# Nine gather slots and two weight slots in a two-layer decoder trunk with product-key expert retrieval

## The reference

```
h = RMSNorm(x);  z = h @ W_in
branches: differential attention, multi-head latent attention, short gated convolution
x += W_out( sum_i sigmoid(gate_i) * (branch_i @ W_branch_i) )
x += PEER(RMSNorm(x))
x += sigmoid(RMSNorm(x) @ W_pg) * (p[layer] @ W_pp)
```

## Time and profile before

| | |
|---|---|
| median of 3 runs | 3571.02 us (3570.99 to 3576.33) |
| the profiled execution | 3578.64 us, its span 3576.8 us |
| TensorE busy | 2852.6 us, 80% |
| VectorE busy | 2525.4 us, 71% |
| POOL, ScalarE busy | 37%, 35% |
| moved by DMA | 1296.91 MB, of it 1073.81 MB gathers and 221.31 MB plain loads |
| mean rate of the DMA | 363 GB/s over the span |

### The profile page before, as it was taken

How to read it: one execution, slowest core, us unless ns; L and a number is a source line. 1 busy time by engine, 2 the same in 40 slices (tenths; PEclk the granted TensorE clock), 3 DMA queues, 4 the chain that set the end, 5 groups by cost and what they waited for, 6 DMA issues and landing times. The chain is left out here.

```text
span 3576.8 us, 28034 instructions
## 1 busy us (share of the span) xinstructions
PE 2852.6 (80%) x8032; PEld 1460.7 (41%) x8032; DVE 2525.4 (71%) x5193; ACT 1263.9 (35%) x3352; POOL 1338.6 (37%) x1033
## 2 busy tenths in 40 slices
PE   8899787778998778777998778878998776557556
PEld 4554634435436334433436334535445432112112
DVE  1411577787777989787767979787767987777775
ACT  2320225456123344456213334447213232223222
POOL 0000033345433444345433443345433344554552
PEclk9989898889999999989999999989999997778777
DMA  4224389899999999999999999899999999999996
GB/s 159 105 83 155 110 339 381 346 415 417 421 421 376 408 410 413 376 403 421 421 418 377 390 411 404 341 406 417 421 421 381 365 409 421 421 422 399 422 422 254
DMA packets 182970, 1296.91 MB, mean 363 GB/s; under 512 B 20384, under 2 KB 21920, under 8 KB 28192
## 3 DMA queue, kind: packets, MB, share of 16 engines
q0 software_dynamic: 147456, 1073.81, 73.2%
q1 hardware_dynamic: 35360, 221.31, 15.7%
HBM read 1292.94 MB, written 2.10 MB: 362 GB/s over the span
## 5 line engine op out<-in xcount | busy, mean ns | idle before, releaser
L595 POOL DMA_INDIRECT ring<-in_uv,experts x1024 | 1336.1, 1305 | 2190.8 <-DVE x L1315 888.1
L1439 PE MATMUL ps_sum<-ring,diag 128*128 128x512 f32 x2008 | 1167.3, 723 | 572.2 <-ACT diag L860 570.3
L1306 DVE SCALAR_TENSOR_TENSOR ring<-ring,h_ffn 128x1024 f32<-128x1024 f32 x1024 | 1234.7, 1221 | 236.7 <-DMA ring<-in_uv,experts 229.8
L1439 PEld LDWEIGHTS ps_sum<-ring,diag 128*128 128x128 f32 x2008 | 416.7, 222 | 1202.4 <-ACT diag L860 827.7
L1315 DVE SCALAR_TENSOR_TENSOR x<-ring,weight,x 128x1024 f32<-128x1024 f32 x522 | 670.1, 1284 | 157.4 <-ACT weight L864 155.1
L858 ACT ACTIVATE diag<-ident,dots 128x128 f32<-128x128 f32 x502 | 200.6, 400 | 705.8 <-DVE ring L1306 693.2
L862 ACT ACTIVATE dots<-dots 128x1 f32<-128x1 f32 x522 | 104.3, 200 | 740.8 <-DVE ring L1306 735.7
L1577 PE MATMUL ps_act<-area_h,wt 128*128 128x256 f32 x1536 | 348.6, 385 | 2.6 <-ACT area_h L611 2.6
L1705 PE MATMUL ps_act<-wt,area_h 128*128 128x512 f32 x768 | 338.3, 594 | 10.2 <-DMA wt<-in_weights 10.2
L1577 PEld LDWEIGHTS ps_act<-area_h,wt 128*128 128x128 f32 x1536 | 294.7, 193 | 61.3 <-issue 18.2
L1501 PE MATMUL ps_act<-wt,area_h 128*128 128x512 f32 (+1 forms) x704 | 299.7, 585 | 4.4 <-ACT area_h L611 4.4
(11 more groups left out here) (193 smaller groups left out, 2152.9 us busy)
## 6 DMA issues: line engine op xcount, KB each, us to landing
wt<-in_weights SPq DMA_DIRECT2D x182, 1024.0 KB
ring<-in_uv,experts POOLq DMA_INDIRECT x1024
wt<-in_weights SPq DMA_DIRECT2D x8, 832.0 KB
wt<-in_weights SPq DMA_DIRECT2D x11, 512.0 KB
wt<-in_weights SPq DMA_DIRECT2D x4, 768.0 KB
x<-in_x SPq DMA_DIRECT2D x4, 512.0 KB, 5.5
area_y<-in_keys SPq DMA_DIRECT2D x4, 512.0 KB
area_f<-in_keys SPq DMA_DIRECT2D x4, 512.0 KB
```

Source lines behind the costliest of these rows:

```text
L595: pool.indirect_dma_start(ring[:, row.slot, :], None, a[f"uv{row.step // 2}"][:, :], bass.IndirectOffsetOnAxis(ap=experts[:, row.step % 2, ...
L1306: dve.scalar_tensor_tensor(u, u, 1.0, h_ffn[:, row.tile, :], ALU.mult, ALU.mult, accum_out=dots[:, row.j:row.j + 1]).then_inc(dots_ready, 1)
L1439: ins = pe.matmul(ps_sum[:, b, :], diag[:, row.pe_before % DIAGS, :], ring[:, row.slot, D + b * 512:D + (b + 1) * 512], start=row.pe_first ...
```

## The change

The ring gets nine slots instead of eight, `wt` two instead of three; both are 8 KB per partition and slot, so the sum is the same. With two slots only two tail tiles can stay in `wt`; the third one (tile 2, half size) goes to the first 1024 columns of `area_kv`, which held keys and values. It is loaded as the last of four tail loads.

```diff
-RING = 8
+RING = 9
...
-W_SLOTS = 3
+W_SLOTS = 2
...
-        tail_wt = [area_t[:, 0:2048], area_b[:, 2048:4096], area_b[:, 4096:5120]]
+        tail_wt = [area_t[:, 0:2048], area_b[:, 2048:4096], area_b[:, 4096:5120], area_kv[:, 0:1024]]
...
-                        load(done // 2, 0, PLE_TILES[:3])
+                        load(done // 2, 0, PLE_TILES[:2])
                         sp.wait_ge(dve_ops, WHERE[("topk", STEPS - 1, 1, len(TOPK_OPS) - 1)].dve + 4)
-                        for i, w in enumerate(tail_wt):
-                            sp.dma_start(w, a["weights"][done // 2, 3 + i, :, 0:PLE_TILES[3 + i]]).then_inc(tail_loaded, 16)
+                        for i, w in zip((3, 4, 5, 2), tail_wt):
+                            sp.dma_start(w, a["weights"][done // 2, i, :, 0:PLE_TILES[i]]).then_inc(tail_loaded, 16)
...
-                for n, w in enumerate((tile(2), tail_wt[2])):
+                for n, w in enumerate((tail_wt[3], tail_wt[2])):
```

## The result

The changed kernel takes **3764.5 us** (median of 4 runs, 3756.6 to 3785.3) against 3572.3 us (4 runs): ratio 1.0546, 95% interval 1.0525 to 1.0567, **+192 us**. The forecast was 3704 with a range of 3605 to 3790. The profiled execution took 3756.63 us with a span of 3754.8, the fastest of the four; against the profiled one of before that is +178.0 us of span.

A forecast was written before the change was run, and what follows sets the result against it. TensorE was taken to lead the mixing stages with the DMA level, the DMA alone the last slices. Head 17, mixing 113, ple_out 7, qkv and out 11, ring -15 gave +133 us on the median 3571.02: 3704 us, range 3605 to 3790.

The forecast's parts named there:

- Head, +17: Head, no gathers: ten new weight-tile stalls of 1.4 us, 14 us, plus 3 us for the early gates.
- Mixing stages, +113: Three mixing stages with gathers: new stalls for branch and second gate tiles plus slow clock, 37.7 us per stage.
- The C wait: Mixing stages with gathers: branch tile lands in 8.0 us, needed after 3.43, so stalls 4.6 us, six per stage.
- B is issued when the branch ends: Mixing stages: second gate tile meets a filled ring, lands in 4.85 us, stalls 1.4 us, five per stage.
- That is 0 or 1.8 us; I take 1.0: Mixing stages: slow clock after each branch-tile stall adds 0 or 1.8 us to the block; 1.0 taken.
- ple_out +7: ple_out, three times: second half's first tile stalls 5.7 us, 2.9 left behind VectorE's cover, 2.4 taken; range 0 to 17.
- qkv and out +11: qkv (twice with gathers) and out (three times): next first half stalls 2.2 us, total +11, range 0 to 19.
- ring -15: Ninth ring slot: one row, 2.5 us, less lost in each DMA rate dip; -15 us, range 0 to -27.
- the cheap case: Rival: all weight tiles land as in the head, 4.85 us; +40 us, about 3611 us; chance 0.14.
- the dearest: Rival: both mixing stalls meet gathers and every branch-tile stall drops the clock; +225 to +265, about 3810 us; chance 0.14.
- signs of a wrong forecast: Branch blocks starting without a wait, unit under 23 us, or DMA rate outside mixing up by several per cent.
- The two in which the DMA leads: Rivals: mixing paced by DMA, hiding TensorE's stalls; -10 to -40, about 3545 us, or cancelling, 3571 within 7; chance 0.04 each.

The follow-up runs named there:

- order_w2r9: Changed kernel, but in the gates both token tiles read the first weight tile, then both the second: ratio 1.0266 to the kernel before, 3665.4 us.
- order_w3r8: Kernel before (three weight slots, eight ring slots), but in the gates both token tiles read the first weight tile, then both the second: 0.9979, 3566.2 us.
- w2r9_again: The changed kernel run once more without an edit, as yardstick for the other runs: ratio 1.0548 to the kernel before, 3773.1 us.
- w2r8: Changed kernel with eight ring slots instead of nine, keeping two weight slots and the moved tail tile: ratio 1.0566 to the kernel before, 3776.0 us.
- w3r7: Kernel before with seven ring slots instead of eight, three weight slots kept: ratio 1.0098 to the kernel before.
- tail_home: Kernel before with only the third tail tile moved to area_kv as last of four loads: ratio 1.001, 3574.9 us.
- warm4: Changed kernel with four unused matmuls before each branch's wait for its weight tile, in steps with gathers: ratio 1.0538 to the kernel before.

## Why the prediction was right, and where it was short

Right: the direction, the mechanism, the places and their order, with the result inside the range and at the upper end of the forecast's own spread (3640 to 3765). The price was 0.69 of what was measured, +133 against +192. Two terms came out near for reasons that were not foreseen; they are called luck below.

- *What bounds the kernel.* TensorE leads the mixing stages with the DMA level: shown. What TensorE loses there, by waits and by slow blocks, goes one for one into the time (order_w2r9: 103 us less of both, 101 us gained), and order_w3r8 removed even the small waits of before.
- *Head, +17.* The end of the head's mixing is 16.9 us late, and that it agrees so well is luck. Right is the stall: ten waits of 1.3 to 1.5 us, 14.2 in sum, for 14 forecast, from a landing read off one row. But five units are 17.3 us longer, 24.0 us each instead of 20.6 (forecast 23.4): with each break about 0.3 us go besides the wait, since the next block no longer overlaps the one before. The early gates cost 5.4 us and not 3: they waited 5.06 us and then ran slow, 16.56 us for 32 records. What hides these 5.4 us is that this execution came to the early gates 5.8 us sooner than the kernel before did, its first blocks having run faster (the last mla_up block starts at 148.52, in the kernel before at 154.28). That is a difference of executions, not of kernels: in w2r9_again the block starts at 154.23, and there the head's mixing ends 21.4 us late. The step that was short is "3 us": it charged no slow clock and no lost overlap.

```profile
148.52 1.88 PE L1669 MATMUL ps_act<-wt,area_f 128*128 128x512 f32 x4
155.45 16.56 PE L1705 MATMUL ps_act<-wt,area_h 128*128 128x512 f32 x32 [5.06 <-DMA wt<-in_weights]
```

- *Mixing stages, +113.* Measured +146.6. This is the term that was too small, and two of its factors were. The waits: 76.7 us before the branches of the three stages and 39.6 before gate blocks, 116.3 in sum, less some 9 that were there before, 107; forecast 18 x 4.6 + 15 x 1.4 - 9 = 95. The C wait was near in the mean (4.3 against 4.6), and that is luck too: the forecast had 18 waits of one kind, 4 to 6 us, and there were twelve of 3.8 to 6.5 and six of 1.4 to 1.7. "One per 2.34 us" holds only within a burst of gathers. Around the row the bursts stand 8 and 11 us apart, in the changed kernel up to 15 us, and a C tile that falls behind such a pause lands in 4.8 to 5.1 us. The step that failed is "B is issued when the branch ends ... the ring has filled by then ... so I take 4.85". That holds from the fourth unit on (0.6 to 1.8 us), but a stage begins with the DMA at its ceiling, and its second and third units paid 5.6 and 2.7 us. The first and the fourth unit of the first stage:

```profile
908.00:940.00 32.00, 26.22 (x58) 11.25 (x57) 17.42 (x23) 5.85 (x19) 12.07 (x8) 0.89 1.01 421
...
998.00:1029.00 31.00, 24.06 (x49) 10.19 (x50) 16.46 (x23) 3.84 (x14) 9.32 (x6) 0.89 0.76 305
```

  The clock: the rest is 146.6 - 107 = 39 us, against 18 x 1.0. Of it 34 us stand in the blocks themselves (26 in the branch blocks above their 7.03 us, 8 in five gate blocks above 10.57); the other 5 fit the overlap lost at each break. The step that failed is "That is 0 or 1.8 us; I take 1.0". A branch block behind a wait of 3.8 to 6.5 us took 8.5 to 9.9 us instead of 7.0, and five gate blocks behind B waits of 2.5 to 5.8 us were slow too (one behind 2.68 was not), for which I had charged nothing. The Trainium skill's page "TensorE: Matmul & The Clock Gate", section "HAM oscillation", with its loop that is cold after every wait for a DMA, was the better guide: behind every branch wait of 3.8 us or more in these stages the block was slow, behind those of 1.4 to 1.7 none. What the prediction called its single case was no test of it: the slow block at 67.71 stood behind small operations with TensorE busy 4.8 of the 6 us, not behind a wait for a DMA, and the earlier trace rows had a block at full speed (10.57 us) behind a DMA wait of 1.45.
- *ple_out +7, qkv and out +11, ring -15.* `out` alone took 13 us, twice my 2.2 us a stage, since its waits of 3 us were longer and in two of the three places brought slow blocks too (15.67 and 15.41 us for 32 records instead of 13.90). The rest came to +1.4 us together, against -4 forecast (7 + 4 - 15), but not by its parts: ple_out alone is 28 us longer on TensorE, where the forecast had 17 (5.7 each) of which 7 were left behind VectorE's cover, and much of it is gone again by the next stage. Of the ring's -15, w2r8 against w2r9_again shows 6, within 0 to 15: right in sign at best, too large in size. The count of dips gives no more than a bound: 11 slices under 400 GB/s in the kernel before, 27 us, for a slot that gave 6; in w3r7 there are 19 between the sixth and the thirty-ninth, 47 us by the same count, for a slot that gave 35.

```profile
GB/s 158 103 83 162 100 357 374 367 393 421 421 421 365 404 398 399 396 383 421 421 406 361 389 397 389 351 378 404 421 417 377 368 393 422 422 422 388 422 422 264
```

- *Tail tile, nothing.* Borne out by tail_home.
- *Rivals.* Neither the cheap case (all at 4.85) nor the dearest (all loaded and cold) came; the stage's beginning was like the second, its end between the two. The DMA rate of the mixing stages, 336 to 350 GB/s, came near the 330 forecast; none of the signs of a wrong forecast appeared. The two in which the DMA leads are refuted by order_w3r8 and by the hollows in the DMA rate.

What is left open: the median of the changed kernel stands 14 us further from before than its profiled execution, and its runs spread over 29 us where those of before spread over 5 in the same comparison. In the later one the spreads are alike (16 us in w2r9_again, 13 in the kernel before). Some 6 of the 14 us are the early start of the profiled execution; the profiled one of w2r9_again, without it, is 195.5 us behind. The rest is not explained, and no run was made for it. Nine ring slots beside three weight slots were not tried either, so the ninth slot's price is known only beside two.

## What to carry to other kernels

The number of slots of a stream is only half of its notice; the order in which the tiles are read is the other half, and it costs nothing. A tile that is read first and third holds its slot for the third reading: reading each tile to its end before the next gave back 100 of 190 us with two slots, and made the kernel with three 0.2% faster than it had been. When a buffer is taken from one stream for another, price both by the wait that they leave (landing time less notice, plus the slow clock behind it) and test the depth in both directions first: here the slot that was bought was worth at most 15 us, and the one that was sold some 200 (w2r8).

## What the runs showed of the hardware that was not expected

- A 1 MB load among queued gathers lands 4.3 us later than alone (9.1 against 4.85), but halving it saves nearly the same in both cases (1.2 to 1.3 and 1.0 to 1.1 us), which is its bytes at the full rate. A load issued right behind another lands one row's 2.5 us plus its own bytes after it (the tail's four loads). The Trainium skill's page "DMA: Bandwidth & Descriptors", section "Queues, rings and completion order", has each engine drain a whole packet of one queue before it turns to the next. The loads that follow another agree with that, one row's share being 2.49 us; the first one does not quite, since its 4.3 us are more than one row.
- Waits of the same length can end at either level of the clock. Behind waits of 1.0 to 1.8 us the next block was at full speed in all the mixing stages of these runs. Behind 2.51 us a gate block of the changed kernel took 12.06 us (976.83) and behind 2.65 us a branch block of warm4 8.83 us (1032.14), both slow; behind 3.41 us a block of order_w2r9 took 7.11 us (930.51), at full speed. Behind every wait of 3.8 us or more in the changed kernel's mixing stages the block was slow.
